# Attention in a two-block kernel: transposing unscaled probabilities by a product with a diagonal of reciprocal sums

## The reference

```python
def one_block(args):
    qn_b, qr_b = args
    s = (jnp.einsum('bqhd,bkhd->bhqk', qn_b, k_nope)
         + jnp.einsum('bqhd,bkd->bhqk', qr_b, k_rope))
    p = jax.nn.softmax(s.astype(jnp.float32) * scale, axis=-1)
    return jnp.einsum('bhqk,bkhd->bqhd', p.astype(v.dtype), v)
```

## Time and profile before

| | |
|---|---|
| median of 3 runs | 3271.42 us (3266.91 to 3272.53) |
| the profiled execution | 3270.7 us, span 3268.9 us |
| PE busy | 3151.0 us (96%) |
| PE weight loads busy | 2539.1 us (78%) |
| DVE busy | 2089.2 us (64%) |
| ACT busy | 1296.5 us (40%) |
| POOL busy | 891.2 us (27%) |
| mean granted TensorE clock | 0.989 |

### The profile page before, as it was taken

The page is one execution under the profiler, slowest core; times in us unless marked ns, Lnnn a source line. Parts: engine busy times, 40 slices in busy tenths (PEclk is TensorE's granted clock), DMA queues, the critical chain, the costliest instruction groups (busy, mean ns, idle before and its releaser), DMA issues.

```text
span 3268.9 us, 61761 instructions
## 1 busy us (share of the span) xinstructions
PE 3151.0 (96%) x26560; PEld 2539.1 (78%) x26560; DVE 2089.2 (64%) x3031; ACT 1296.5 (40%) x2289; POOL 891.2 (27%) x778
## 2 busy tenths in 40 slices
PE   8989998999999988999999999999999999999998
PEld 8678777788888776467888888878677878888887
DVE  5363465666766665847899887762455475565686
ACT  4333334555555432124333344443333343333444
POOL 1232243232222222100577740000000026666100
PEclk9999999999999999999999999999999999999999
DMA  4251245111211221632132247522102322322753
GB/s 151 68 160 46 71 172 167 41 45 61 71 56 44 79 82 46 214 126 91 71 114 108 97 157 246 167 92 92 39 27 80 130 84 90 116 100 97 265 160 116
DMA packets 128016, 346.46 MB, mean 106 GB/s; under 512 B 15792, under 2 KB 19520, under 8 KB 124928
## 3 DMA queue, kind: packets, MB, share of 16 engines
q1 hardware_dynamic: 106592, 258.09, 24.0%
q0 software_dynamic: 21152, 84.42, 6.9%
HBM read 246.51 MB, written 95.94 MB: 105 GB/s over the span
## 4 chain that ended last, share of the span: by engine, by line
PE 85%; DVE 8%; ACT 4%; issue 2%; DMA 1%; POOL 1%; SPq 0%; DVEq 0%; ACTq 0%; POOLq 0%
PE ps L369 43%; PE ps L368 39%; PE ps L372 4%; DVE AR L378 2%; DVE X L378 2%; DVE SM L389 1%; DVE WS L378 1%; DVE W L378 1%; ACT AR L375 1%; DVE HT L382 1%; ACT WS L375 0%; ACT W L2226 0%; ACT X L375 0%; ACT HT L1245 0%; POOL AR L378 0%
## 5 line engine op out<-in xcount | busy, mean ns | idle before, releaser
L378 DVE TENSOR_TENSOR WS<-W,WS 128x512 fp32r<-128x512 f32 (+1 forms) x284 | 342.1, 1205 | 250.2 <-ACT WS L375 250.0
L368 PE MATMUL ps<-HH,WS 128*128 128x512 f32 x1280 | 394.3, 390 | 0.0
L368 PE MATMUL ps<-TO,WS 128*128 128x512 f32 x1440 | 346.0, 390 | 0.0
L375 ACT ACTIVATE WS<-W 128x512 fp32r<-128x512 f32 (+1 forms) x284 | 210.0, 739 | 315.5 <-PE ps L369 170.8
L368 PEld LDWEIGHTS ps<-TO,WS 128*128 128x128 f32 x1440 | 270.5, 188 | 55.9
L368 PEld LDWEIGHTS ps<-HH,WS 128*128 128x128 f32 x1280 | 240.4, 188 | 49.7
L368 PE MATMUL ps<-HL,WS 128*128 128x512 f32 x640 | 249.3, 390 | 0.0
L368 PE MATMUL ps<-TO 128*128 128x512 f32 x936 | 227.0, 390 | 0.2 <-DVE TO L378 0.2
L369 PE MATMUL ps<-AR 64*64 64x64 f32 (+2 forms) x5440 | 205.2, 244 | 22.3 <-ACT AR L375 11.0
L368 PE MATMUL ps<-WS 128*128 128x512 f32 x888 | 215.2, 390 | 0.1
L375 ACT ACTIVATE X<-ps 128x512 f32<-128x512 f32 (+1 forms) x168 | 100.3, 597 | 285.3 <-PE ps L369 129.1
(11 more groups left out here) (367 smaller groups left out, 6417.7 us busy)
## 6 DMA issues: line engine op xcount, KB each, us to landing
AR_b<-h_d SPq DMA_DIRECT2D x154, 256.0 KB, 2.9
AR<-rw_d SPq DMA_DIRECT2D x104, 256.0 KB, 4.2
W<-in_w_fg SPq DMA_DIRECT2D x44, 512.0 KB, 3.9
W<-in_w_fu SPq DMA_DIRECT2D x44, 512.0 KB, 5.0
h_d<-FST POOLq DMA_DIRECT2D x20, 1024.0 KB, 4.4
x_d<-X POOLq DMA_DIRECT2D x24, 512.0 KB, 4.6
W<-in_w_tok SPq DMA_DIRECT2D x24, 512.0 KB, 4.4
rw_d<-X POOLq DMA_DIRECT2D x40, 256.0 KB, 3.4
```

What stands on the lines that cost most here:

```text
L368: return pe.e.matmul(o, l, r, start=start, stop=stop, skip_group_check=True)
L375: return e.e.activation(o, x, ACT.Copy)
L378: return e.e.tensor_tensor(o, x, y, op)
```

## The change

The exponentials are no longer scaled in place. DVE scales the 128x128 identity by the column of reciprocal sums instead, into one of two new tiles `DG` at the free end of HT, and PE transposes each piece of the unscaled probabilities by a plain product, the piece as weights and the diagonal as the moving operand, so that the output is the transposed piece with each query's column scaled. Waits and signals stay where they were.

```diff
@@ -1090,6 +1090,7 @@
         AVH = [v3(HT[:, 4096 + 512 * i:4608 + 512 * i], 8) for i in range(2)]
         APB = [HT[:, 5120 + 1024 * i:6144 + 1024 * i] for i in range(2)]
         AOT = [OTB, HT[:, 7168:7680]]
+        DG = [HT[:, 7680 + P * i:7680 + P * (i + 1)] for i in range(2)]
 
         def apt(i):
             return (W1[:, 0:1024], W1[:, 1024:2048], SC[0].spare, SC[1].spare)[i % 4]
@@ -1197,7 +1198,8 @@
                     b = take(pe, "pT", i, g, banks=MAIN)
                     pe.wait_ge(*at("ve_att", "p", i))
                     for j in range(4):
-                        x = tr(pe, ps[:, b, j * P:(j + 1) * P], APB[i % 2][:, (4 * g + j) * P:(4 * g + j + 1) * P])
+                        x = mm(pe, ps[:, b, j * P:(j + 1) * P], APB[i % 2][:, (4 * g + j) * P:(4 * g + j + 1) * P], DG[i % 2],
+                               True, True)
                     x.then_inc(*pe.sig("pe_att", "pT", i, g))
 
             def pv(m):
@@ -1217,7 +1219,7 @@
                 ve.wait_ge(*at("ae_att", "p", i))
                 ve.e.reciprocal(rs, rs).then_inc(*ve.sig("ve_att", "inv", i))
                 ve.wait_ge(*at("ve_att", "inv", i))
-                ts(ve, APB[i % 2], APB[i % 2], rs, None, ALU.mult, None).then_inc(*ve.sig("ve_att", "p", i))
+                ts(ve, DG[i % 2], ident, rs, None, ALU.mult, None).then_inc(*ve.sig("ve_att", "p", i))
             return att_steps(skip, scale, skip, skip)
 
         def att_ve(ve):
```

## The result

The changed kernel takes 3319.55 us in the median of 4 runs (3317.75 to 3320.50), against 3269.64 us before (4 runs): 49.9 us more, a ratio of 1.0152 with a 95% interval of 1.0134 to 1.0169. It is slower, by nearly the amount forecast (3318). The profiled execution took 3320.5 us, with a span of 3318.7.

A forecast was written before the change was run, and what follows sets the result against it. The prediction took PE, 94% busy in the attention stretch, as the bound: 56.7 us of added records less 4 for DVE's relief and 5 for other waits is 47.7, on 3270.7 giving 3318 us; 8-of-10 range 3297 to 3335.

The forecast's parts named there:

- PE bounds the stretch: Attention window 545 to 1130 us: PE is busy 94% and sets the time, with small waits of 30.2 us.
- The second record, 0.111 us, 56.7 us in all: Attention transposes: each of 512 pieces as plain float32 product leaves a second matmul record, adding 56.7 us of PE work.
- DVE's relief, 4 us: Smaller scaling on DVE returns time only where PE waited for it; 4 us taken back.
- The bound of 4.7: PE's 9 waits for the scaling, each result 0.53 us earlier: at most 4.7 us back.
- to keep the stretching: DVE scaling: its 9.7 us of being held up, as beside POOL, was assumed to remain.
- Other waits, 5 us: PE's other 21.5 us of waits in the attention stretch: a quarter, 5 us, comes back.
- ACT follows without setting a bound: ACT's copies after the transposes move up to 0.89 us later; 53% busy, ACT has room and adds no bound.
- rival 2: Attention stretch: nothing comes back and the longer turn opens new waits on ACT; 56.7 to 65.3 us more; chance 0.13.
- Rival 1: PE's waits in the attention stretch swallow more of the added work; only 27 to 36 us more; chance 0.18.
- rival 3: A tile's 16 records: a pair streams in 0.110 us, no PE time added, 3265 us; chance 0.05.
- Rival 4: Attention pieces: product costs four times the transpose, 4 x 0.110 us each, 169 us more, 3440; chance 0.02.
- The sum: Whole kernel: 56.7 - 4 - 5 = 47.7 us more, giving 3318 us, slower by 1.5%.

The follow-up runs named there:

- the run with transposes: Changed kernel with the small identity scaling kept but pieces transposed with the plain identity, result unscaled: 3262.16 us, ratio 0.9977.
- The run with fp32r: Changed kernel with exponentials and diagonal written as fp32r, rounded float32, so each product leaves one record: 3265.36 us, ratio 0.9991.
- the run with the identity product: Kernel before, probabilities still scaled in place, but each piece transposed by a plain product with the identity: 3321.77 us, ratio 1.0164.
- the half and the double dose: Changed kernel with only 4 of 8 pieces through the diagonal product: 3288.72 us; with each piece going through it twice: 3427.96 us.
- the constant factor: Small scaling with plain transposes, its factor a constant in the instruction instead of a column in SBUF: 3265.18 us, one run.

## Why the prediction was right, step by step

- **PE bounds the stretch.** Right. Three doses of records (256, 512 and 1536 above the run with transposes) cost 0.104, 0.107 and 0.108 us each. There is no free first part and no bend that the noise, some 5 us, would let one see.
- **The second record, 0.111 us, 56.7 us in all.** Right in kind and nearly in size: 0.112 between starts. Counted from the first start to the next group's first, it is 0.92 us a tile and 58.9 us; the prediction read that figure for its 4-product group (0.98 against 0.96) but that group, too, has 8 records and says nothing of 16. The run with fp32r shows that the second record is the whole price.
- **DVE's relief, 4 us.** About right: 4.6 us less waiting in the trace, 4.9 us between the run with the identity product and the changed kernel, 6.5 where the transposes stayed. The bound of 4.7, argued from PE's idle time, was met beside the long turn and perhaps passed without it (6.5, by the interval 4.6 to 10.5). The expected 34 us less of DVE work are 33.3 in the page, and part of that is luck: the scaling itself lost 58.0 - 27.9 = 30.1 us, and a second profile of the changed kernel has DVE at 2061.2 us, 28.0 less than before. The error inside is the small scaling, which takes 0.288 us and not 0.227: the row that I took adds a constant (line 744), where this one reads its factor from SBUF. It made no difference that can be seen. And to keep the stretching was right: 64 x (0.436 - 0.288) = 9.5 us of it are left, of 9.7.
- **Other waits, 5 us.** They gave 3.4. As argued, most of them don't shrink, since ACT's copies and the next exponential move along with the transposes.
- **ACT follows without setting a bound.** Right. Its waits for the transposes into `W` rose:

```profile
ACT W L375 <- PE ps L369: 114.1, 105, 4.3
```

(545 to 1180; this row also holds the waits for other products of line 369, 8.9 us before, which stood apart from the 71.3 us of the earlier trace rows: so 80.2 became 114.1). PE's wait for the exponential is 4.0 us where it was 3.5: rival 2's new waits did not come.

- **The rivals.** Rival 2's other half, that nothing comes back, fell with the 8.0 us less of waits. Rival 1 (27 to 36 us) and rival 3 (a pair in 0.110 us) fell with the half and the double dose. Rival 4 asked for 0.44 us a piece; the ratio of the product to the transpose is two, not four. The Trainium skill's advice in "Perfetto Trace Analysis", section "Transposes", to use the transpose operation for a logical transpose, held for the float32 product, which cost 49.9 us here; the fp32r product kept the pace of the transposes (0.94 us a tile for 0.96).
- **The sum.** It was 47.7 us and the change cost 49.9. The trace has 2.2 us more of record time and 1.0 less back, which would give 50.9; the last 1 us is within the noise. The list of PE's waits in the earlier trace rows holds 57 waits, not 56, and nothing hangs on it.

## What to carry to other kernels

Folding a scale into a transpose trades vector time for matmul records, and in float32 each piece needs a second record; where TensorE is busy 94% of a stretch, 30 us of VectorE work were worth little more than the waits that they caused (6.5 us, of which 4.1 show as shorter waits), and each added record its full spacing. Count the records of a plain float32 product in the same trace, of the same weight width, before replacing a transpose. If a column scale is wanted, try it where the tile is smallest: here on the 64-wide output, with the reciprocals spread by a product of half width, 128 records in place of 512.

## What was not expected of the hardware

A 128x128 scaling on VectorE takes 227 ns with a constant factor and 288 with a factor read from SBUF. And making it an eighth as wide did not make it proof against POOL. In the changed kernel, timeline from 871:

```profile
870.49 1.11 POOL L1282 DMA_DIRECT2D oa_d<-HT  x2 [1.60 <-ACT HT L375]
...
871.44 3.05 DVE L382 TENSOR_SCALAR HT<-CS,SM 128x128 f32<-128x128 f32 x1
871.62 2.11 POOL L378 TENSOR_TENSOR AR<-AR,CS 128x256 f32<-128x256 f32 x3
873.69 0.71 POOL L378 TENSOR_TENSOR QF<-AR,QF 96x256 fp32r<-96x256 f32 x1
...
874.55 1.78 PE L369 MATMUL ps<-HT 128*128 128x128 f32 x10 [1.75 <-DVE HT L382]
```

The 0.29 us operation took 3.05, and ended 0.09 us after POOL's last one (874.49 against 874.40). The 128x1024 one at 732.76 got through earlier, between POOL's third and fourth operation: it ended at 735.54, 0.62 us after the third:

```profile
733.89 1.03 POOL L378 TENSOR_TENSOR AR<-EX 128x512 f32<-128x512 f32 x1
```

PE waited 1.75 us for the scaling at 871.44, the longest of the three waits that make up the 4.1 us left. It is a pattern: of the 64 small scalings in this trace 17 took over 0.35 us, and POOL was at work when each of the 17 began; 16 of them ended 0.08 to 0.14 us after a POOL operation did, the other beside three POOL operations that the row joins. Of the 47 shorter ones 5 overlap POOL. The maximum is the same, 3.05 us, for the constant factor. The longest fell from 3.51 us before to 3.05, by 0.46, which is the difference of the two medians (0.754 - 0.288): the shorter operation saves its own part, and not the time for which it is held up.

The Trainium skill has a rule for this, in "SBUF — State Buffer", section "Who interferes with whom": a VectorE operation in a two-port mode and a GpSimd operation contend for a shared pair of ports, the first to issue gets it for its whole instruction, and the other is blocked until then. The trace agrees in that the scaling ends just behind a POOL operation, and in that one which began before POOL (940.99, against 941.13) took its usual 0.29 us. It shows no mode of the scaling. And at 871.44 the only POOL work under way was a DMA issue, yet the scaling stood through the four operations that began after it; an issue at 632.38 did not hold one up (632.51, 0.29 us). Why it waits for several operations in a row stays open; a kernel in which POOL's work is moved away from the scaling was not tried.
